# Seven products over whole contraction halves, with weight operations of eight tiles

## The chip, the core and the metric

The kernel runs on one core of a Trainium2 chip. The metric is the time on the device in microseconds, the median of the runs.

## What is computed

One step of a decoder layer on 512 prompt tokens and 8 sample tokens (520 columns in all, `TC`). The normalised input is projected by one wide matrix, and two branches read the result: dilated window attention (three groups of eight heads of 128) and chunkwise retention (eight heads, keys and values of 256). Their outputs are gated, projected, merged, projected again, normed and added to the residual; then comes a gated per-layer embedding. All is float32.

```python
u = rms_norm(h, g_pre)
z = jnp.einsum('bsd,de->bse', u, w_in)                 # 2048 x 22528
qa, ka, va, za, qr, kr, vr, zr, ga, gb = jnp.split(z, split_points, axis=-1)
...
merged = (jax.nn.sigmoid(ga) * jnp.einsum('bse,ed->bsd', ya, w_a_out)
          + jax.nn.sigmoid(gb) * jnp.einsum('bse,ed->bsd', yr, w_r_out))
y = jnp.einsum('bsd,de->bse', merged, w_o)
h = h + rms_norm(y, g_post)
h = h + jax.nn.sigmoid(jnp.einsum('bsd,de->bse', h, w_ple_gate)) * jnp.einsum('bsp,pd->bsd', p, w_ple_proj)
```

## The kernel before

**Splitting.** Every float32 operand of a matmul is split into a high part, rounded to the type that TensorE multiplies (`F32R`), and a low part, the rest. A product takes three passes: high by high, high by low, low by high. ScalarE makes the high part of the weights with a copy (`hi`, line 1004), VectorE the low part by subtraction (`lo`, line 1395). The moving operand (`U`, `V`) is split once for each stage.

**Pairs and operations.** The projections run over pairs of column blocks of 128 (`pairs`): five pairs a head for attention (numbers 0 to 39: q0 q1, k0 k1, q2 k2, v0 v1, v2 z), four a head for retention (q, k, v, gate z), sixteen for the gates, then the plain stages (`w_a`, `w_r`, `w_o`, the embedding's projection and gate). A pair is a list of operations (`OPS`); each is a weight tile of 4 x 128 columns that `hi` and `lo` split into one of `AHEAD` = 6 slots of `W`, and that TensorE then uses. SyncE loads the raw weights of a pair into `raw`, one buffer for one pair, in two halves of the contraction (`load`, lines 488 and 492); a half is loaded again when the low part of the last operation that reads it has been made.

**Seven products.** An `S` pair multiplies a 2 x 2 block form in seven products in place of eight (two column blocks by two halves of the 520 columns, and two parts of the contraction). Here this form covers the contraction's second half alone: tiles 8 to 11 against 12 to 15. Operations 0 to 6 are the seven products, 12 matmuls of 260 columns each; operations 7 to 10 are the first half in the plain form, 24 matmuls each: 180 in all, where a plain pair (`F`, `N`) has 192. Sums of weights are made by VectorE (lines 1390, 1392, 1399, 1402), sums of the moving operand once, at the start. ScalarE copies three partial results out of the accumulator (`part`, line 1061); VectorE adds them when it evicts the tiles (lines 1470, 1503).

**Order.** Each engine's order is written out by hand. For each operation n of a pair, VectorE and ScalarE run `steps`: what must be evicted, then the side work hung on that step (`hooks`), then `lo` or `hi` of the operation `AHEAD` places on. TensorE runs its own hooks ahead of the product of the same number: transposes, scores, values. Side work on VectorE includes the sample tokens' key products (`sample_keys`, lines 1640, 1643), softmax maxima and normalisation, state updates of the samples (`sample_states`, from line 1767), the retention's output (`ret_output`, from line 1821) and sample value columns (`sample_columns`, line 1734). GpSimd issues the loads and stores of the stages. SyncE issues the weight loads and, after each pair's, one or two copies of cache rows of 1 MB.

## Time and profile before

| | us |
|---|---|
| runs | 2926.57, 2930.59, 2932.53 |
| median | 2930.59 |
| span of the profiled execution | 2924.6 |
| attention pairs, about | 33.5 to 1000 |
| retention pairs, about | 1000 to 1866 |
| gate pairs | 1866 to 2223.6 |
| plain stages | 2223.6 to 2924.6 |

The profiled execution's own time is not given beside its span; the lowest run is 2.0 us above the span, the median 6.0. A row of the profile names the source line, the engine (PE is TensorE, PEld its weight load, DVE VectorE, ACT ScalarE, POOL GpSimd, SP SyncE; a q stands for the sequencer that issues or waits), the operation, what it writes and reads, and the shape. Where an idle time is shown, the arrow names what ended it.

### The profile page before, as it was taken

Reading aid. Unit: us, or ns where it says so; the run is one execution under the profiler, and the core shown is the slowest. Engines: PE = TensorE matmul, PEld = TensorE weight load, DVE = VectorE, ACT = ScalarE, POOL = GpSimd, SP = SyncE. Lnnn points to the kernel's source line nnn. Section 1 sums busy time; section 2 is a strip of 40 time slices with the busy share of each in tenths; the row PEclk is TensorE's granted clock in tenths of the full one; section 3 lists DMA queues with packets and bytes.
Section 4 is the critical chain, followed back from the end, with each engine's and each line's share of the span. In section 5 each row is a group of like instructions: output and inputs, shape, how many; then the busy total and the mean of one; then the engine's idle time right before and its main releaser. Section 6 shows DMA issues by size and latency. Waiting matters only on the chain.

```text
span 2924.6 us, 57340 instructions
## 1 busy us (share of the span) xinstructions
PE 2881.1 (99%) x23566; PEld 2843.2 (97%) x23566; DVE 1761.6 (60%) x3199; ACT 1143.6 (39%) x2078; POOL 350.1 (12%) x516
## 2 busy tenths in 40 slices
PE   7999999999999999999999999999999999999998
PEld 7999999999999999999999999999999999999998
DVE  6666667667666666576666667666654433433732
ACT  5444444444344434434434434433443322333432
POOL 2010000100001002112112112110001100000300
PEclk9999999999999999999999999999999999999999
DMA  8465655656556455456456456577568755553442
GB/s 273 129 211 172 216 169 186 212 163 198 185 186 200 150 173 189 152 202 224 140 200 223 143 197 223 171 271 261 203 230 311 245 195 203 213 184 137 159 163 95
DMA packets 375886, 567.16 MB, mean 194 GB/s; under 512 B 16112, under 2 KB 336432, under 8 KB 372416
## 3 DMA queue, kind: packets, MB, share of 16 engines
q1 hardware_dynamic: 334440, 428.38, 42.6%
q0 software_dynamic: 41184, 135.10, 14.9%
q8 instruction: 187, 3.06, 0.4%
q14 instruction: 75, 0.61, 0.1%
HBM read 511.42 MB, written 228.16 MB: 253 GB/s over the span
## 4 chain that ended last, share of the span: by engine, by line
PE 90%; DVE 4%; DMA 3%; DVEq 1%; ACT 1%; issue 1%; SPq 0%; POOL 0%; ACTq 0%; POOLq 0%
PE acc L546 58%; PE acc L558 21%; PE aux L756 1%; DMA raw_weights<-in_w_in 1%; PE aux L767 1%; DVE weights L1395 1%; PE aux L777 1%; PE aux L844 1%; PE aux L651 1%; DMA stage_buffers<-in_x_prompt 1%; PE aux L712 0%; PE aux L659 0%; DVE stage_buffers L2007 0%; PE aux L681 0%; PE aux L834 0%
## 5 line engine op out<-in xcount | busy, mean ns | idle before, releaser
L546 PE MATMUL acc<-moving,weights 128*128 128x260 f32 x12384 | 1566.1, 284 | 1.9 <-DVE sampled L1470 1.7
L546 PEld LDWEIGHTS acc<-moving,weights 128*128 128x128 f32 x12384 | 1509.4, 188 | 9.7 <-issue 6.1
L1395 DVE TENSOR_TENSOR weights<-raw_weights,weights 128x512 fp32r<-128x512 f32 (+1 forms) x1030 | 709.6, 694 | 599.3 <-ACT weights L1004 562.1
L1004 ACT ACTIVATE weights<-raw_weights 128x512 fp32r<-128x512 f32 (+1 forms) x1030 | 641.1, 626 | 1073.1 <-PE acc L546 439.5
L558 PE MATMUL acc<-moving,weights 128*128 128x260 f32 x5376 | 654.1, 284 | 6.1 <-DVE moving L1458 4.0
L558 PEld LDWEIGHTS acc<-moving,weights 128*128 128x128 f32 x5376 | 650.2, 189 | 6.4 <-issue 4.1
L546 PE MATMUL acc<-combined_moving,weights 128*128 128x260 f32 x3096 | 422.5, 286 | 0.8 <-DVE partial_sums L1503 0.8
L546 PEld LDWEIGHTS acc<-combined_moving,weights 128*128 128x128 f32 x3096 | 389.0, 189 | 1.4 <-DVE weights L1395 1.0
L1470 DVE SCALAR_TENSOR_TENSOR stage_buffers<-acc,partial_sums 128x260 f32<-128x260 f32 x344 | 146.6, 479 | 172.4 <-PE acc L546 172.4
L1004 ACT ACTIVATE weights<-combined_weights 128x512 fp32r<-128x512 f32 x172 | 108.1, 629 | 298.1 <-PE acc L546 268.9
L1061 ACT ACTIVATE partial_sums<-acc 128x260 f32<-128x260 f32 x258 | 99.7, 386 | 239.4 <-PE acc L546 234.3
L1395 DVE TENSOR_TENSOR weights<-combined_weights,weights 128x512 fp32r<-128x512 f32 x172 | 118.5, 689 | 118.5 <-ACT weights L1004 116.8
L2061 POOL DMA_DIRECT2D out<-stage_buffers x70 | 48.2, 689 | 870.9 <-ACTq L1074 657.1
L1390 DVE TENSOR_TENSOR combined_weights<-raw_weights 128x512 f32<-128x512 f32 x86 | 59.6, 693 | 51.9 <-DMA raw_weights<-in_w_in 45.3
L2138 POOL DMA_DIRECT2D out<-stage_buffers x64 | 45.7, 718 | 265.3 <-DVEq L1778 257.7
L1402 DVE TENSOR_TENSOR raw_weights<-raw_weights,combined_weights 128x512 f32<-128x512 f32 x86 | 59.5, 692 | 8.7 <-issue 0.9
L1392 DVE TENSOR_TENSOR raw_weights<-raw_weights 128x512 f32<-128x512 f32 x86 | 59.5, 692 | 8.4 <-issue 0.4
L1399 DVE TENSOR_TENSOR combined_weights<-combined_weights,raw_weights 128x512 f32<-128x512 f32 x86 | 59.5, 692 | 8.0
L2128 POOL DMA_DIRECT2D stage_buffers<-in_state_ret x64 | 45.6, 717 | 127.8 <-DVEq L1784 59.7
L1767 DVE SCALAR_TENSOR_TENSOR stage_buffers<-stage_buffers,sampled 128x256 f32<-128x256 f32 x128 | 53.4, 479 | 1.0
L2247 POOL TENSOR_TENSOR stage_buffers<-stage_buffers 128x520 f32<-128x520 f32 x16 | 24.3, 1520 | 224.8 <-DVE stage_buffers L2007 224.8
L2088 POOL DMA_DIRECT2D stage_buffers<-in_cache_win x24 | 21.7, 904 | 228.2 <-DVE sample_keep L1643 148.8
(264 smaller groups left out, 1873.2 us busy)
## 6 DMA issues: line engine op xcount, KB each, us to landing
out<-in_cache_win SPq DMA_DIRECT2D x128, 1023.5 KB, 8.8
raw_weights<-in_w_in SPq DMA_DIRECT2D x96, 1024.0 KB, 5.9
raw_weights<-in_w_in SPq DMA_DIRECT2D x160, 512.0 KB, 5.3
out<-in_cache_win SPq DMA_DIRECT2D x32, 1022.0 KB, 9.1
out<-stage_buffers POOLq DMA_DIRECT2D x120, 256.0 KB, 3.0
stage_buffers<-in_cache_win POOLq DMA_DIRECT2D x48, 512.0 KB, 5.6
stage_buffers<-in_state_ret POOLq DMA_DIRECT2D x64, 256.0 KB, 4.4
raw_weights<-in_w_r_out SPq DMA_DIRECT2D x16, 1024.0 KB, 5.6
```

The costliest lines, as they stand in the source:

```text
L546: mm = pe.matmul(acc[:, m, half, 0:HC], W[:, g % AHEAD, wp, kk, :], mov(up, kk), start=(start and kk == 0 and n == 0), stop=(stop and kk = ...
L558: mm = pe.matmul(acc[:, m, half, 0:HC], W[:, g % AHEAD, wp, kk, :], moving(first, half)(up, kk), start=(start and kk == 0 and n == 0), sto ...
L1004: act.activation(W[:, g % AHEAD, 0, 0:src.shape[1]], src, ACT.Copy).then_inc(s_whi, 1)
L1061: act.activation(part[:, i, :], acc[:, m, 1, 0:HC], ACT.Copy, scale=scale_of(p)).then_inc(s_read, 1)
L1390: dve.tensor_tensor(tmp_w[:], raw_chunk(2, 0), raw_chunk(3, 0), ALU.add).then_inc(s_sum, 1)
L1392: dve.tensor_tensor(raw_chunk(2, 0), raw_chunk(2, 1), raw_chunk(2, 0), ALU.subtract).then_inc(s_sum, 1)
L1395: dve.tensor_tensor(W[:, g % AHEAD, 1, 0:src.shape[1]], src, W[:, g % AHEAD, 0, 0:src.shape[1]].bitcast(F32), ALU.subtract).then_inc(s_wre ...
L1399: dve.tensor_tensor(tmp_w[:], tmp_w[:], raw_chunk(2, 1), ALU.subtract).then_inc(s_sum, 1)
L1402: dve.tensor_tensor(raw_chunk(3, 1), raw_chunk(3, 1), tmp_w[:], ALU.subtract).then_inc(s_sum, 1)
L1470: return dve.scalar_tensor_tensor(out=out, in0=bank, scalar=scale, in1=other_part, op0=ALU.mult, op1=ALU.add)
L1767: dve.scalar_tensor_tensor(out=r_st[:, slot, b, j, :], in0=r_v[:, slot, b, :], scalar=zs[:, at:at + 1], in1=r_st[:, slot, b, j, :], op0=AL ...
L2061: pool.dma_start(dst, src).then_inc(stored, 16)
```

## The change

The seven-product form of an `S` pair covers the whole contraction: tiles 0 to 7 against 8 to 15. A pair has seven operations of eight tiles, 24 matmuls each, 168 in all; the four plain operations go. The third pair of head 0 becomes plain (`N`), since the sums of the moving operand, now twice as large, are made in the first three pairs.

Every weight operation, in the plain stages too, is of 8 x 128 = 1024 columns; `AHEAD` is 3. `hi` waits for the high part of its slot to be used (`s_hused`) and `lo` for the whole slot. TensorE runs the sixteen matmuls with the high part first, and then waits for the low part. The sums of weights are made in place, in the raw buffer, one after each of the first four low parts. The raw buffer is loaded in four units (half, column block), each when its last reader is done.

VectorE evicts each accumulator when it is complete, in steps 4, 5 and 6. The hooks are moved to the seven (or four) steps that are left. The moving tiles are made in the order 0 to 15 (before: 8 to 15 first), and the first pair reads all eight tiles of a half in each operation. The stage buffers shrink from 15,824 to 12,804 columns: turned probabilities overwrite the probabilities, the attention output its gate, the retention's rows and outputs their sources, two key buffers serve for three. The scratch space for DMA descriptors is set to 4096 bytes. In the embedding's projection an operation serves four output tiles, in the first two pairs of its gate two.

```diff
-OPS = {"S": [("raw", 2, 1), ("raw", 2, 0), ("sum", 0), ("raw", 3, 1), ("sum", 0), ("raw", 3, 1), ("raw", 3, 0),
-             ("raw", 0, 0), ("raw", 1, 0), ("raw", 0, 1), ("raw", 1, 1)],
-       "N": [("raw", c, m) for m in range(2) for c in range(4)],
-       "Q": [("quad", c, t) for c in range(2) for t in range(4)],
-       "F": [("raw", c, m) for c in (2, 3, 0, 1) for m in range(2)],
-       "P": [("two", n // 8, n % 8) for n in range(KD)],
-       "A0": [("raw", c, m) for m in range(2) for c in (0, 1)],
-       "A1": [("raw", c, m) for m in range(2) for c in (2, 3)]}
-AHEAD = 6
+EIGHT = 8
+OPS = {"S": [(0, 1), (0, 1), (0, 0), (0, 1), (0, 1), (1, 0), (1, 1)],
+       "F": [(0, 0), (0, 1), (1, 0), (1, 1)],
+       "N": [(0, 0), (1, 0), (0, 1), (1, 1)],
+       "Q": [(0, 0), (0, 1), (1, 0), (1, 1)],
+       "P": [(0, 0), (0, 1), (1, 0), (1, 1)],
+       "A0": [(0, 0), (0, 1)],
+       "A1": [(1, 0), (1, 1)]}
+AHEAD = 3
...
-            add_pair("F" if h == 0 and j < 2 else "S", w_in, cols)
+            add_pair("FNN"[j] if h == 0 and j < 3 else "S", w_in, cols)
...
-    W = stack.enter_context(nc.sbuf_tensor("weights", [P, AHEAD, 2, 4, P], F32R))
+    W = stack.enter_context(nc.sbuf_tensor("weights", [P, AHEAD, 2, EIGHT, P], F32R))
...
-    POOL_F = 15824
...
+    POOL_F = 12804
...
-    V = stack.enter_context(nc.sbuf_tensor("combined_moving", [P, 2, 3, 4, HC], F32R))
-    tmp_w = stack.enter_context(nc.sbuf_tensor("combined_weights", [P, 4, P], F32))
+    V = stack.enter_context(nc.sbuf_tensor("combined_moving", [P, 2, 3, EIGHT, HC], F32R))
...
+    ya_out = silu_z[:, 0:T]
...
+    LAST_READ = {"S": {unit(0, 0): 2, unit(0, 1): 4, unit(1, 0): 5, unit(1, 1): 6},
...
+        def load(p, u):
+
+            half, m = divmod(u, 2)
+            if read_until[p.nth, u] >= 0:
+                sp.wait_ge(s_wready, read_until[p.nth, u] + 1)
...
+            sp.dma_start(chunk(half, m), rows[:, :, p.cols[m]:p.cols[m] + P]).then_inc(s_wload[u], 16)
...
         def product(g, m, half, mov, start, stop):
 
-            for kk in range(4):
-                for n, (wp, up) in enumerate(passes):
-                    mm = pe.matmul(acc[:, m, half, 0:HC], W[:, g % AHEAD, wp, kk, :], mov(up, kk),
-                                   start=(start and kk == 0 and n == 0), stop=(stop and kk == 3 and n == 2),
-                                   skip_group_check=True)
-            return mm
+            out = acc[:, m, half, 0:HC]
+            pe.wait_ge(s_whi, g + 1)
+            for kk in range(EIGHT):
+                for up in range(2):
+                    mm = pe.matmul(out, W[:, g % AHEAD, 0, kk, :], mov(up, kk), start=(start and kk == 0 and up == 0),
+                                   stop=False, skip_group_check=True)
+            mm.then_inc(s_hused, 1)
+            pe.wait_ge(s_wready, g + 1)
+            for kk in range(EIGHT):
+                mm = pe.matmul(out, W[:, g % AHEAD, 1, kk, :], mov(0, kk), start=False, stop=(stop and kk == EIGHT - 1),
+                               skip_group_check=True)
+            mm.then_inc(s_used, 1)
...
+            n = run(0)
+            if first:
+                pe.wait_ge(s_accfree[0], 1 + p.nth)
+            else:
+                pe.wait_ge(s_bankfree, p.sums)
+            product(n, 0, 1, moving(0, 0), True, False)
+            n = run(1)
+            acc_ready(0)
+            if first:
+                pe.wait_ge(s_comb, 4)
+            product(n, 0, 0, combined(1), True, False)
+            n = run(2)
+            acc_ready(1)
+            if first:
+                pe.wait_ge(s_comb, 8)
+            product(n, 1, 1, moving(0, 1), True, False)
+            n = run(3)
+            pe.wait_ge(s_read, 3 * p.sums + 1)
+            product(n, 0, 1, combined(0), False, True)
+            n = run(4)
+            pe.wait_ge(s_read, 3 * p.sums + 2)
+            product(n, 1, 1, moving(8, 1), False, True)
+            n = run(5)
+            pe.wait_ge(s_read7, p.sums + 1)
+            product(n, 0, 0, combined(2), False, True)
+            n = run(6)
+            product(n, 1, 0, moving(8, 0), True, True)
...
-            src = source(g)
-            act.activation(W[:, g % AHEAD, 0, 0:src.shape[1]], src, ACT.Copy).then_inc(s_whi, 1)
+                act.wait_ge(s_wready, g - AHEAD + 1)
+                act.wait_ge(s_hused, g - AHEAD + 1)
+            for u in units_read(p, n):
+                act.wait_ge(s_wload[u], loads_due[p.nth, u])
+            if p.mode == "S" and 1 <= n <= 4:
+                act.wait_ge(s_sum, 4 * p.sums + n)
+            act.activation(slot(g, W[:, g % AHEAD, 0]), source(g), ACT.Copy).then_inc(s_whi, 1)
...
+                hi(g + n + AHEAD)
+                if p.mode == "S" and n in (0, 2, 3):
                     act.wait_ge(s_used, g + n + 1)
                     if n == 0:
                         act.wait_ge(s_accfree[1], 1 + p.nth)
-                    i, m = {0: (1, 0), 2: (0, 1), 4: (2, 0)}[n]
+                    i, m = {0: (1, 0), 2: (0, 1), 3: (2, 0)}[n]
                     act.activation(part[:, i, :], acc[:, m, 1, 0:HC], ACT.Copy, scale=scale_of(p)).then_inc(s_read, 1)
...
-            strassen = p.mode == "S"
-            if strassen and n == 0:
-                dve.wait_ge(s_wload[1], 16 * loads_due[p.nth, 1])
-                dve.drain()
-                dve.tensor_tensor(tmp_w[:], raw_chunk(2, 0), raw_chunk(3, 0), ALU.add).then_inc(s_sum, 1)
-                dve.drain()
-                dve.tensor_tensor(raw_chunk(2, 0), raw_chunk(2, 1), raw_chunk(2, 0), ALU.subtract).then_inc(s_sum, 1)
-            src = source(g)
+            if g >= AHEAD:
+                dve.wait_ge(s_used, g - AHEAD + 1)
             dve.wait_ge(s_whi, g + 1)
-            dve.tensor_tensor(W[:, g % AHEAD, 1, 0:src.shape[1]], src, W[:, g % AHEAD, 0, 0:src.shape[1]].bitcast(F32),
+            dve.tensor_tensor(slot(g, W[:, g % AHEAD, 1]), source(g), slot(g, W[:, g % AHEAD, 0]).bitcast(F32),
                               ALU.subtract).then_inc(s_wready, 1)
-            if strassen and n == 2:
-                dve.drain()
-                dve.tensor_tensor(tmp_w[:], tmp_w[:], raw_chunk(2, 1), ALU.subtract).then_inc(s_sum, 1)
-            if strassen and n == 3:
-                dve.drain()
-                dve.tensor_tensor(raw_chunk(3, 1), raw_chunk(3, 1), tmp_w[:], ALU.subtract).then_inc(s_sum, 1)
+            if p.mode == "S":
+                weight_sums(p, n)
+
+        def weight_sums(p, n):
+
+            first, other = chunk(0, 1), chunk(0, 0)
+            if n == 0:
+                dve.wait_ge(s_wload[unit(0, 0)], loads_due[p.nth, unit(0, 0)])
+                dve.tensor_tensor(first, first, other, ALU.subtract).then_inc(s_sum, 1)
+            if n == 1:
+                dve.wait_ge(s_wload[unit(1, 0)], loads_due[p.nth, unit(1, 0)])
+                dve.tensor_tensor(other, other, chunk(1, 0), ALU.add).then_inc(s_sum, 1)
+            if n == 2:
+                dve.tensor_tensor(first, chunk(1, 0), first, ALU.subtract).then_inc(s_sum, 1)
+            if n == 3:
+                dve.wait_ge(s_wload[unit(1, 1)], loads_due[p.nth, unit(1, 1)])
+                dve.tensor_tensor(first, chunk(1, 1), first, ALU.subtract).then_inc(s_sum, 1)
...
+                    if n == 4:
+                        dve.wait_ge(s_read, 3 * s + 3)
+                        dve.wait_ge(s_read7, s + 1)
+                        evict(p, 0, 1, tiles[0], scale).then_inc(s_bankfree, 1)
+                    if n == 5:
+                        dve.wait_ge(s_used, g + 5)
+                        evict(p, 1, 1, tiles[1], scale)
+                    if n == 6:
+                        dve.wait_ge(s_used, g + 6)
+                        tile_ready(p, 0, tiles[0], scale)
...
+                if p.mode == "S" and n == 6:
+                    dve.wait_ge(s_used, g + 7)
+                    tile_ready(p, 1, tiles[1], scale)
+                lo(g + n + AHEAD)
...
+            return {(1, 0): [lambda: sample_states(0, h)], (1, 4): [lambda: sample_ret_y(0, h), lambda: sample_states(1, h)],
+                    (2, 0): [lambda: sample_ret_y(1, h)], (2, 1): [lambda: sample_states(2, h)], (2, 4): [lambda: sample_ret_y(2, h)],
+                    (3, 2): [lambda: sample_states(3, h)], (3, 6): [lambda: sample_ret_y(3, h)]}
...
-    nc = bacc.Bacc("TRN2", target_bir_lowering=False, num_devices=1)
+    nc = bacc.Bacc("TRN2", target_bir_lowering=False, num_devices=1, dynamic_dma_scratch_size=4096)
```

## Rows read from the trace of the kernel before

**Rows 1.** Page, part 1: span; each engine's busy time, share, instructions.

```profile
span 2924.6 us, 57340 instructions
PE 2881.1 (99%) x23566; PEld 2843.2 (97%) x23566; DVE 1761.6 (60%) x3199; ACT 1143.6 (39%) x2078; POOL 350.1 (12%) x516
```

**Rows 2.** Page, part 4: chain that ended last, shares by engine.

```profile
PE 90%; DVE 4%; DMA 3%; DVEq 1%; ACT 1%; issue 1%; SPq 0%; POOL 0%; ACTq 0%; POOLq 0%
```

**Rows 3.** Windows: length, busy PE, PEld, DVE, ACT, POOL; clock, DMA share, GB/s.

```profile
276.00:396.57 120.57, 120.57 (x1007) 120.26 (x1006) 79.25 (x144) 51.50 (x103) 9.41 (x14) 1.00 0.60 188
...
1648.80:1757.55 108.75, 108.41 (x860) 104.59 (x859) 75.31 (x152) 41.46 (x72) 21.64 (x32) 1.00 0.56 189
...
1866.00:2223.60 357.60, 357.06 (x2988) 356.65 (x2987) 224.53 (x402) 152.91 (x274) 33.34 (x49) 1.00 0.67 238
```

**Rows 4.** Windows of line 546 alone (PE, PEld): five gate pairs.

```profile
2115.91:2223.64 107.73, 107.73 (x902) 107.69 (x900) 1.00 0.62 225
```

**Rows 5.** Timeline, first projection: start us, length us, engine, line, operation, idle before.

```profile
32.74 0.69 DVE L1458 TENSOR_TENSOR moving<-stage_buffers,moving 128x520 fp32r<-128x520 f32 x1
...
33.58 26.60 PE L558 MATMUL acc<-moving,weights 128*128 128x260 f32 x206 [4.00 <-DVE moving L1458]
...
34.02 0.69 DVE L1458 TENSOR_TENSOR moving<-stage_buffers,moving 128x520 fp32r<-128x520 f32 x1
```

**Rows 6.** VectorE groups by shape: count, busy us, mean ns, idle before.

```profile
L1395 DVE TENSOR_TENSOR weights<-raw_weights,weights 128x512 fp32r<-128x512 f32 x1014 | 699.8, 695 | 590.9 <-ACT weights L1004 554.1 <-issue 0.7
...
L1640 DVE TENSOR_TENSOR stage_buffers<-stage_buffers 128x1024 f32<-128x1024 f32 x24 | 29.3, 1221 | 1.1
...
L1470 DVE SCALAR_TENSOR_TENSOR stage_buffers<-acc,partial_sums 128x260 f32<-128x260 f32 x298 | 125.5, 457 | 172.4 <-PE acc L546 172.4
```

**Rows 7.** ScalarE groups by shape, same columns.

```profile
L1004 ACT ACTIVATE weights<-raw_weights 128x512 fp32r<-128x512 f32 x1014 | 634.5, 629 | 1064.4 <-PE acc L546 439.5 <-PE acc L558 348.3 <-DVE raw_weights L1392 130.1
...
L1122 ACT ACTIVATE combined_moving<-stage_buffers 128x1040 fp32r<-128x1040 f32 x3 | 3.2, 1065 | 1.2 <-DVEq L1535 1.2
...
L1145 ACT ACTIVATE stage_buffers<-stage_buffers,sample_keep 128x1024 f32<-128x1024 f32 x32 | 36.5, 1141 | 17.0 <-DMA stage_buffers<-vrow_scr 17.0
```

**Rows 8.** The same timeline in one attention pair.

```profile
312.68 0.69 DVE L1392 TENSOR_TENSOR raw_weights<-raw_weights 128x512 f32<-128x512 f32 x1
...
313.29 0.68 DVE L1395 TENSOR_TENSOR weights<-raw_weights,weights 128x512 fp32r<-128x512 f32 x1
...
313.48 0.63 ACT L1004 ACTIVATE weights<-raw_weights 128x512 fp32r<-128x512 f32 x1 [0.97 <-DVE raw_weights L1392]
...
314.15 0.69 DVE L1395 TENSOR_TENSOR weights<-raw_weights,weights 128x512 fp32r<-128x512 f32 x1 [0.18 <-ACT weights L1004]
```

**Rows 9.** Loads: L492 at 86.0, at 305.1, all; L488, 1000 to 1866.

```profile
DMA to landing us min/median/max: 4.1/4.1/4.1
...
DMA to landing us min/median/max: 4.9/4.9/4.9
...
DMA to landing us min/median/max: 3.8/5.3/17.9
...
DMA to landing us min/median/max: 4.9/6.3/12.2
```

**Rows 10.** The same timeline: VectorE in a retention head.

```profile
1665.51 0.68 DVE L1821 COPY stage_buffers<-aux 128x512 f32<-128x512 f32 x1
...
1669.01 0.69 DVE L1395 TENSOR_TENSOR weights<-combined_weights,weights 128x512 fp32r<-128x512 f32 x1
...
1675.28 1.67 DVE L1767 SCALAR_TENSOR_TENSOR stage_buffers<-stage_buffers,sampled 128x256 f32<-128x256 f32 x4
...
1678.71 1.29 DVE L1395 TENSOR_TENSOR weights<-raw_weights,weights 128x512 fp32r<-128x512 f32 x2
...
1735.71 2.35 DVE L1734 TENSOR_TENSOR stage_buffers<-stage_buffers,sample_keep 128x1024 f32<-128x1024 f32 x2
...
1739.49 0.69 DVE L1395 TENSOR_TENSOR weights<-raw_weights,weights 128x512 fp32r<-128x512 f32 x1
```

755 lines of the change are left out of this document (377 added, 378 removed).

## The prediction

> **What bounds the kernel now.** I read the page's busy times first, then the chain of waits, then windows by stage, and last the single instructions around one pair of column blocks. TensorE is busy 99% of the span [rows 1] and carries 90% of the chain that ended last [rows 2]. Its clock is granted in full (1.00, the 2.4 GHz level) in an attention head, a retention head and the gate stage [rows 3]. Five gate pairs in a row without other TensorE work take 107.73 us for 900 matmuls [rows 4]: 0.1197 us a matmul, 21.55 us a pair of 180. So today a matmul removed is time removed. VectorE is busy 66% of an attention head and 69% of a retention head [rows 3]. The question is what becomes of that reserve when each weight operation grows to 1024 columns and half as many are held ahead.
>
> **The removed matmuls.** Before: 86 S pairs of 180 matmuls and 2 F pairs of 192, 15,864 in all. After: 85 S pairs of 7 x 24 = 168 and 3 plain pairs of 192, 14,856. That is 1,008 fewer, and 1,008 x 0.1197 = 120.7 us if TensorE stays the bound. A gate pair would then take 20.1 us. By the same rate five attention pairs (120.57 us before) come to 113.4, four retention pairs (108.75) to 103.0, sixteen gate pairs (357.6) to 334.6 [rows 3]. The matmuls of the later plain stages stay the same in number.
>
> **The first pair.** Tiles of the moving operand come every 1.28 us while the first projection runs (32.74 to 34.02) [rows 5]. Today each group of four tiles is used twice before the next is wanted, and the pair ends near 58.4 (192 of the 206 matmuls of the row that begins at 33.58). Afterwards the first operation wants eight tiles at once. The eighth is there at 33.4 + 7 x 1.28 = 42.4; its last two matmul pairs and the 16 low-part matmuls end at 44.8; three operations of 48 x 0.1197 = 5.75 follow, which find the sixteenth tile (52.6) in time: 62.0. Cost: 3.6 us.
>
> **The new loop.** The weight buffer holds one pair, and the four sums now stand in a line: each overwrites what the operation before has read. Between two pairs there is a closed loop. The low part of operation 4 ends, so the block of half 0, column 1 may be loaded for the next pair; then its high part (ScalarE), low part (VectorE), first sum (VectorE), high part, low part, second sum, and so on, to the low part of operation 4 again. That is one load, 5 high parts, 5 low parts, 4 sums. Today the loop holds a load too, but operations of 512 columns (0.63 and 0.69 us [rows 6, 7]), and the long products of half 0 cover it.
>
> The prices: a VectorE operation over 1024 columns 1.22 us (line 1640) [rows 6]; a ScalarE copy of 1040 columns into the rounded type 1.07 us, one of 1024 with a scale in place 1.14 [rows 7] (I take 1.06, being of the first kind, and keep 1.14 as the bound); a low part followed by a sum overlaps by 0.08 (312.68 + 0.69 against 313.29); from VectorE's end to ScalarE's start 0.11, back 0.04 [rows 8]. A load of 512 KB alone lands in 4.1 us, beside a cache copy in 4.9; the median of all is 5.3, but half of those stand behind another [rows 9]. I take 4.4, nearest to the undisturbed one, and keep 4.1 and 5.3. Sum: 4.4 + 5 x 1.06 + 9 x 1.22 - 4 x 0.08 + 6 x 0.11 + 5 x 0.04 = 21.2 us a pair, between 20.9 and 22.5. It lies above the 20.1 of a gate pair and just under the 21.55 of today: in the gates the loop takes nearly all of the gain. The Trainium skill (DMA: Bandwidth & Descriptors, Anatomy of one DMA) fits, for the software path, 2.0 us plus bytes over 436 GB/s, an estimated 3.2 us for such a load, which would make the loop 20.0 and leave TensorE the bound; the row's 4.1 speaks against it.
>
> **What else VectorE does in the loop.** While ScalarE makes a high part, VectorE is free for 0.11 + 1.06 + 0.04 = 1.21 us, four times a pair; two of these gaps are taken up by evictions (0.46 us each and more, line 1470) [rows 6]. While the load runs, it is free for about 5.6 us less two low parts and two evictions, 2.4 us. Side work that does not fit its gap lengthens the loop.
> - Attention, a head: a sample-key product and reduction, 2 x 1.22, in one gap: 1.2 over. Two bursts of about 5 us (maxima with a key product; exchange with normalisation, an estimate from the 1024-column price) in the load's gap: 2 x 2.6. Small things 1: in all 7.4. Loop 5 x 21.2 + 7.4 = 113.4, TensorE 113.4. Two bounds as close as that do not meet in every pair, since VectorE can run ahead of TensorE by two products at most; I take 115.5, 5.1 less than before. Seven heads: -36. Head 0: two S pairs -2; its third pair becomes plain, +1.4.
> - Retention, a head [rows 10]: a state update is 3.4 us (1675.28 to 1678.71): 2.2 over in an empty gap, 3.5 with scaled keys beside it, 1.2 in the load's gap. The output step is 3.5 (1665.51 to 1669.01) in a gap that evictions have filled: 3.4 over. Update and sample columns, 3.4 + 3.8 (1735.71 to 1739.49), in the load's gap: 4.8. The last columns 2.5. In all 17.6. Loads of 1 MB in this stage land in 6.3 where undisturbed ones take 4.9 [rows 9]; half of that, 0.7, for each half-size load. Loop 4 x 21.9 + 17.6 = 105.2, TensorE 103.0; with the same lack of fit 106, 2.7 less than before. Eight heads: -22.
> - Gates: 16 x 21.2 + 21 (one output step 3.4, four updates 5, columns 8, the closing tiles 5) = 360, 3 more than before.
>
> **Edits with one answer.** SyncE issues four loads of half the size for a pair; what waits behind them are cache copies, for which nothing waits before the end. The copies of partial sums on ScalarE now follow the next high part: product 4 starts one high part and one copy (1.5 us) after its own high part, which fits, as TensorE has 1 us a pair to spare where the loop binds and is not late where it doesn't. The denser stage buffers (turned probabilities and outputs over their sources, two key buffers for three) wait for stores that end a pair or more earlier; nothing where GpSimd keeps up, and it is busy 12% of the span [rows 1]; up to 2 us a head if one store is late. Less room for GpSimd's DMA descriptors shows in no row; I take nothing.
>
> **Sum.** -36 - 2 + 1.4 - 22 + 3 + 3.6 = -52. The profiled span is 2924.6; the three runs lie 2.0 to 7.9 above it, their median 6.0. So 2872.6 + 6.0 = 2879 us, 1.8% faster.
>
> **Rivals.**
> - *TensorE stays the bound.* Loads that land sooner once each has the queue to itself, and side work that fits better than I count, give -120.7 + 3.6 = -117: 2813. For it: loop and TensorE differ by only one us a pair. Against: the 4.1 us.
> - *The loop is longer and the kernel slower.* At the upper prices (load 5.3, high part 1.14) the loop is 22.5: attention 5 x 22.5 + 7.4 = 120 a head (nothing won), retention 4 x 23.2 + 17.6 = 110.4 (+1.6 x 8 = 13), gates 16 x 22.5 + 21 = 381 (+23), start +3.6: about +40, 2970. It decides from about 21.8 us a pair, 0.6 above my price: 52 us over 83 S pairs. For it: one weight buffer, so that each microsecond of a load is paid in the loop, and loads in this program wait for one another. The Trainium skill (Trainium Kernel Development and Optimization, Best Practices) says to double-buffer so that DMA overlaps with compute; this change loads into a buffer that the last sums have only just left, and by that rule this rival is what happens.
> - *Late stores*: the buffers shared in the stages cost 2 us in each of 16 heads on top of the forecast, 2911: still faster.
>
> **How the numbers follow.** Chances: forecast 0.47 (2850 to 2915), TensorE the bound 0.22, longer loop 0.21, late stores 0.10. The range takes in the first rival and part of the second: 2811 to 2945. A measurement tells about 0.2% (6 us) from no change. Faster: the forecast, the first rival and the third, less a little at the edge, 0.76; within 0.2%, the loop near 21.8, 0.06; slower 0.18.
>
> **What would show it.** If I am right, gate pairs without side work take about 21 us, TensorE waits there about a microsecond a pair for ScalarE's high parts, and ScalarE's longest waits are for the weight load and for VectorE's sums. Attention pairs lose about 1 us each, retention pairs 0.7. The first pair ends near 62. If TensorE stays the bound, gate pairs take 20.1 and nothing waits. If the loop is longer, gate pairs take over 21.6. I am wrong about the loop if the load is not waited for, or if ScalarE's 1024-column copy or VectorE's operations are not near 1.06 and 1.22 us.

## The result, and the profile after

The change made the kernel slower. The changed kernel takes 3071.6 us (median of 4 runs, 3071.3 to 3072.9), the kernel before, run beside it, 2929.6: a ratio of 1.0486 [1.0471, 1.0501], 142 us more. The prediction had said 2879, with a range that ended at 2945.

The page of the changed kernel (busy times, then the chain that ended last) answers [rows 1, 2]:

```profile
span 3069.6 us, 54404 instructions
PE 2845.6 (93%) x22558; PEld 2779.5 (91%) x22558; DVE 1992.9 (65%) x2727; ACT 1158.6 (38%) x1600; POOL 350.5 (11%) x517
...
PE 49%; DVE 23%; ACT 9%; DMA 6%; DVEq 6%; issue 6%; ACTq 1%; POOL 1%; SPq 0%; POOLq 0%
```

The 1,008 matmuls are gone (23,566 to 22,558 instructions). But TensorE now stands idle for 3069.6 - 2845.6 = 224 us, where it was 43.5, and carries 49% of the chain that ended last, where it was 90%. Its busy time fell by 35.5 us and not by the 120.7 of the removed matmuls. Of the other 85 us at most some 64 are work done at the lower clock (1.2 GHz): TensorE is busy for 138 us in the stretches granted that level, for 10 before, and half of the difference is the most that it can cost. The rest must be short waits inside rows that count as busy: the gate pairs below are busy for 82.55 us at a clock of 1.00, where the same matmuls take 80.64 in a later run. Windows (columns as in [rows 3]): an attention head, that head's second pair (called j1 from here on; the pairs of a head are j0, j1 and so on), a retention head, the gates, and four gate pairs without side work:

```profile
543.76:670.43 126.67, 115.69 (x947) 114.79 (x946) 93.48 (x124) 53.55 (x82) 9.41 (x14) 0.97 0.58 182
568.81:598.49 29.68, 21.08 (x175) 20.88 (x173) 21.42 (x25) 9.18 (x11) 2.89 (x4) 0.92 0.72 205
1644.46:1761.05 116.59, 107.32 (x811) 101.22 (x810) 87.46 (x136) 43.52 (x57) 21.63 (x32) 0.96 0.56 176
1990.40:2360.10 369.70, 348.67 (x2831) 342.54 (x2830) 264.14 (x334) 159.92 (x212) 34.10 (x50) 1.00 0.68 230
...
2251.07:2335.83 84.76, 82.55 (x674) 81.09 (x673) 58.87 (x64) 36.53 (x49) 2.86 (x4) 1.00 0.66 224
```

Undisturbed gate pairs take 84.76 / 4 = 21.19 us, the 21.2 of the forecast. The attention head, though, went from 120.6 to 126.7, the retention head from 108.8 to 116.6, the gates from 357.6 to 369.7 [rows 3] (their window is laid 5 us early), and in the heads the granted clock is 0.96 or 0.97 on average. By stages, each from its first product to the next one's, attention takes 1018.6 us, retention 943.2, the gates 369.8 and the plain stages 704.3: about 52, 77, 12 and 3 more than before. The forecast had -33, -22, +3 and 0, so retention missed by some 99 us and attention by 85. What TensorE waited for, the largest four (us in total, times, longest):

```profile
PE aux L689 <- DVEq L1560: 72.0, 15, 8.9
PE aux L805 <- DVE sample_keep L1859: 35.3, 7, 5.5
PE aux L786 <- DVEq L1560: 21.0, 7, 8.1
PE aux L882 <- DVEq L1855: 14.7, 18, 2.4
```

None of them is a product of the projections. They are transposes of an evicted tile (L689 in attention, L786 in retention), the second values product of retention (L805) and its products with the sampled states (L882), each waiting for VectorE. The longest, at the end of that attention pair j1, in the timeline of all engines:

```profile
575.59 1.22 DVE L1471 TENSOR_TENSOR raw_weights<-raw_weights 128x1024 f32<-128x1024 f32 x1
576.72 1.22 DVE L1713 TENSOR_TENSOR stage_buffers<-stage_buffers 128x1024 f32<-128x1024 f32 x1
578.02 1.22 DVE L1716 TENSOR_REDUCE sample_keep<-stage_buffers 128x8 f32<-128x1024 f32 x1
579.15 2.35 DVE L1453 TENSOR_TENSOR weights<-raw_weights,weights 128x1024 fp32r<-128x1024 f32 x2
...
588.86 1.23 DVE L1713 TENSOR_TENSOR stage_buffers<-stage_buffers 128x1024 f32<-128x1024 f32 x1 [5.47 <-DMA stage_buffers<-row_scr]
...
589.98 1.06 ACT L1056 ACTIVATE weights<-raw_weights 128x1024 fp32r<-128x1024 f32 x1 [9.03 <-DMA raw_weights<-in_w_in]
...
597.72 1.11 PE L689 MATMUL aux<-ident,stage_buffers 128*128 128x128 f32 x4 [8.60 <-DVEq L1560]
598.49 3.20 PE L575 MATMUL acc<-moving,weights 128*128 128x260 f32 x16
```

Two things wait for a DMA at once. VectorE waits 5.47 us for the second set of sample keys (L1713), and ScalarE waits 9.03 us for the next pair's weights (L1056). Both loads were let go by VectorE within 1.2 us of each other: the reduction at 578.02 frees the key buffer, the remainder at 579.15 (that is, a low part) frees the weights' block. The issues of 577 to 583, KB each, median us to landing:

```profile
raw_weights<-in_w_in SPq DMA_DIRECT2D x2, 512.0 KB, 9.7
stage_buffers<-in_cache_win POOLq DMA_DIRECT2D x1, 512.0 KB, 6.6
```

9.7 is the median of two weight loads; the first, issued at 580.39, is the one that ScalarE waits for and took 9.5 us. I had it at 4.4, 5.3 at most. After such a gap the first 16 matmuls take 3.20 us, where 2.09 to 2.17 is usual in this trace.

### The profile page after: what moved, and what is told of

Read it like the earlier page. It is cut to its first block, busy times and chain, and to the rows that moved or that the text cites. A ratio compares the mean times of both kernels' runs of the same rounds, so it can differ in the third digit from the quotient of the medians.

```text
span 3069.6 us, 54404 instructions
## 1 busy us (share of the span) xinstructions
PE 2845.6 (93%) x22558; PEld 2779.5 (91%) x22558; DVE 1992.9 (65%) x2727; ACT 1158.6 (38%) x1600; POOL 350.5 (11%) x517
## 3 DMA queue, kind: packets, MB, share of 16 engines
q1 hardware_dynamic: 488360, 428.39, 43.5%
## 4 chain that ended last, share of the span: by engine, by line
PE 49%; DVE 23%; ACT 9%; DMA 6%; DVEq 6%; issue 6%; ACTq 1%; POOL 1%; SPq 0%; POOLq 0%
PE acc L575 14%; PE acc L592 13%; DVE weights L1453 11%; ACT weights L1056 7%; PE acc L598 7%; PE acc L580 6%; DMA raw_weights<-in_w_in 3%; DVEq L1560 3%; DVE raw_weights L1463 2%; DMA stage_buffers<-row_scr 2%; DVE stage_buffers L1533 1%; PE aux L805 1%; DVE raw_weights L1471 1%; DVE raw_weights L1468 1%; PE aux L815 1%
## 5 line engine op out<-in xcount | busy, mean ns | idle before, releaser
L1453 DVE TENSOR_TENSOR weights<-raw_weights,weights 128x1024 fp32r<-128x1024 f32 x723 | 884.6, 1226 | 851.7 <-ACT weights L1056 489.4
L1056 ACT ACTIVATE weights<-raw_weights 128x1024 fp32r<-128x1024 f32 x723 | 761.7, 1058 | 1647.0 <-PE acc L592 318.8
L575 PE MATMUL acc<-moving,weights 128*128 128x260 f32 x5440 | 750.0, 292 | 11.5 <-ACT partial_sums L1114 11.4
L575 PEld LDWEIGHTS acc<-moving,weights 128*128 128x128 f32 x5440 | 703.5, 195 | 18.2 <-ACT partial_sums L1114 15.0
L575 PE MATMUL acc<-combined_moving,weights 128*128 128x260 f32 x4080 | 544.4, 286 | 8.2 <-DVE stage_buffers L1533 5.1
L575 PEld LDWEIGHTS acc<-combined_moving,weights 128*128 128x128 f32 x4080 | 508.5, 189 | 11.2 <-DVE stage_buffers L1533 7.0
L592 PE MATMUL acc<-moving,weights 128*128 128x260 f32 x3712 | 473.3, 286 | 14.0 <-DVE stage_buffers L1533 7.7
L592 PEld LDWEIGHTS acc<-moving,weights 128*128 128x128 f32 x3712 | 457.4, 190 | 16.7 <-DVE stage_buffers L1533 7.9
L580 PE MATMUL acc<-moving,weights 128*128 128x260 f32 x2720 | 387.8, 286 | 0.0
L580 PEld LDWEIGHTS acc<-moving,weights 128*128 128x128 f32 x2720 | 356.6, 192 | 0.0
L580 PE MATMUL acc<-combined_moving,weights 128*128 128x260 f32 x2040 | 286.6, 283 | 0.0
L580 PEld LDWEIGHTS acc<-combined_moving,weights 128*128 128x128 f32 x2040 | 262.9, 189 | 0.0
L598 PE MATMUL acc<-moving,weights 128*128 128x260 f32 x1856 | 242.5, 283 | 0.0
L598 PEld LDWEIGHTS acc<-moving,weights 128*128 128x128 f32 x1856 | 232.1, 189 | 0.0
L1533 DVE SCALAR_TENSOR_TENSOR stage_buffers<-acc,partial_sums 128x260 f32<-128x260 f32 (+1 forms) x340 | 160.9, 473 | 79.9 <-PE acc L580 70.1
L2146 POOL DMA_DIRECT2D out<-stage_buffers x70 | 48.3, 690 | 944.9 <-ACTq L1123 711.9
L1466 DVE TENSOR_TENSOR raw_weights<-raw_weights 128x1024 f32<-128x1024 f32 x85 | 103.5, 1218 | 5.2 <-DMA raw_weights<-in_w_in 5.2
L1471 DVE TENSOR_TENSOR raw_weights<-raw_weights 128x1024 f32<-128x1024 f32 x85 | 103.5, 1218 | 0.0
L1468 DVE TENSOR_TENSOR raw_weights<-raw_weights 128x1024 f32<-128x1024 f32 x85 | 103.5, 1218 | 0.0
L1463 DVE TENSOR_TENSOR raw_weights<-raw_weights 128x1024 f32<-128x1024 f32 x85 | 103.5, 1218 | 0.0
L689 PE MATMUL aux<-ident,stage_buffers 128*128 128x128 f32 x192 | 34.0, 306 | 72.7 <-DVEq L1560 72.0
```

The source lines that it names most:

```text
L575: mm = pe.matmul(out, W[:, g % AHEAD, 0, kk, :], mov(up, kk), start=(start and kk == 0 and up == 0), stop=False, skip_group_check=True)
L580: mm = pe.matmul(out, W[:, g % AHEAD, 1, kk, :], mov(0, kk), start=False, stop=(stop and kk == EIGHT - 1), skip_group_check=True)
L592: mm = pe.matmul(acc[:, m, half, 0:HC], W[:, g % AHEAD, 0, kk, :], moving(first, half)(up, kk), start=(start and kk == 0 and up == 0), sto ...
L598: mm = pe.matmul(acc[:, m, half, 0:HC], W[:, g % AHEAD, 1, kk, :], moving(first, half)(0, kk), start=False, stop=(stop and kk == EIGHT - 1 ...
L1056: act.activation(slot(g, W[:, g % AHEAD, 0]), source(g), ACT.Copy).then_inc(s_whi, 1)
L1453: dve.tensor_tensor(slot(g, W[:, g % AHEAD, 1]), source(g), slot(g, W[:, g % AHEAD, 0]).bitcast(F32), ALU.subtract).then_inc(s_wready, 1)
```

## The experiments

Two theories stood at the start. **A**: what was added stands in VectorE's queue (the key product behind its wait, then weight operations, then the evictions), and TensorE's side work waits for its end. **B**: the closed chain of the weights (load, rounding on ScalarE, remainder and sum on VectorE, again rounding) sets the pairs. After four runs B was worked out as **D**: a pair takes the chain's 21.3 us plus whatever lengthens one of its links.

**Key products moved apart.** In VectorE's tables, attention:

```diff
-                {1: [lambda: sample_keys(0, h - 1)], 4: [lambda: sample_keys(1, h - 1)]} if h else
+                {1: [lambda: sample_keys(0, h - 1)]} if h else
...
-                 3: [lambda: sample_keys(2, h - 1)], 5: [lambda: masked_far(1, h)]} if h else
+                {0: [lambda: sample_keys(1, h - 1)], 1: [lambda: masked_near(0, h)],
...
-                {**({} if h else {0: [first_lo], 2: [lambda: masked_far(1, h)]}),
+                {**({0: [lambda: sample_keys(2, h - 1)]} if h else {0: [first_lo], 2: [lambda: masked_far(1, h)]}),
```

> The changed kernel with one thing moved: VectorE's second key product of each attention head goes from step 4 of the key pair (j1) to step 0 of the next pair (j2), the third from step 3 of j2 to step 0 of j3, so that some six steps lie between two products that share one buffer, where there were three. Theory A (what was added stands in VectorE's queue: it waits 4 to 6 us for the key load, the next pair's weight operations and the evictions stand behind that wait, and TensorE's transposes at step 0 of j2 wait 8 us for an eviction): TensorE's wait there falls from 8 us to under 1 us in each of 7 heads (-50 us), the half clock that follows it goes too (-20 us), pair j1 falls from 29.1 to 21.5-22.5 us, the time from 3072 to about 3000 (2985-3020). Theory B (the closed chain of load, rounding, remainder and sum sets the pairs, wherever the key products stand): pairs as before the move, 3072 within 0.3%. Theory C (the wait only moves along, to j2 or j3): j1 gets shorter by 7, j2 and j3 together longer by 4 or more, about 3045.

Measured: 3078.9 us (two runs, 3072.1 and 3085.8). TensorE's wait stayed:

```profile
PE aux L689 <- DVEq L1560: 74.4, 15, 9.0
```

VectorE no longer waits for keys in j1, yet nothing is won. The wait that I had read off first, the 5.47 us, was not the one that counted: ScalarE's 9 us for the weights end 1.1 us later, and with the keys out of the way the wait for the weights is still there (9.47 us in the same head). Theory A fell for attention.

**State products read early.** In TensorE's table and in VectorE's:

```diff
-                    (2, 3): [lambda: sample_states(0)], (3, 5): [lambda: sample_states(1)]}
+                    (2, 3): [lambda: sample_states(0)], (3, 4): [lambda: sample_states(1)]}
...
-                    (3, 2): [lambda: sample_states(3, h)], (3, 6): [lambda: sample_ret_y(3, h)]}
+                    (3, 2): [lambda: sample_states(3, h)], (3, 4): [lambda: sample_ret_y(3, h)]}
```

> The changed kernel with one thing moved: in retention's fourth pair (j3) TensorE's products with the sampled states go from step 5 to step 4 and VectorE's copy of them out of the bank from step 6 to step 4. Theory A (TensorE's second values product at step 6 waits 5 us for that copy, which stands behind two remainders and two sums of the next pair's weights on VectorE): the wait goes from 5.0 to under 1 us in 7 heads (-35 us), the half clock behind it goes (-15 us), pair j3 falls from 36.2 to 29-31 us, the time from 3072 to about 3022 (3005-3040). Theory B (the closed weight chain sets j3): unchanged within 0.3%. Theory C (TensorE waits for the next thing in VectorE's queue in its place, the sampled rows or the value columns): j3 falls by under 2 us, over 3055.

Measured: 3026.5 us, -45. The same j3 in windows of the changed kernel and of this one:

```profile
1723.88:1761.05 37.17, 32.05 (x220) 28.80 (x219) 24.71 (x33) 11.16 (x16) 3.25 (x5) 0.91 0.37 116
```

```profile
1701.00:1731.07 30.07, 30.07 (x221) 27.88 (x220) 24.74 (x33) 11.18 (x16) 3.17 (x5) 1.00 0.45 140
```

The wait at L805 is gone, TensorE is busy without a break, and the clock is back at the upper level. This third of the loss was a hook's place: VectorE freed bank 3 at step 6, behind two remainders and two sums of the next pair, and TensorE wanted it at step 6. Here A holds.

**Both moves.**

> Both moves of the two runs before together. Theory A: the gains add, -70 and -50: about 2952 (2925-2990), so that most of the 142 us that the change lost, or all of it, is gone with no weight operation removed. Theory B: 3072. If only one of the two waits cost time: 3000 or 3022.

Measured: 3029.4 us (ratio to before 1.0341 [1.0323, 1.0358]): the second move's gain and nothing from the first.

**TensorE kept busy in the wait.** Before the wait of the transposes at step 0 of j2:

```diff
+            for _ in range(75):
+                pe.transpose(aux[:, 3, 0:P], ident[:], ident[:])
             pe.wait_ge(s_zT, tiles)
```

> The changed kernel with 75 transposes of the unit matrix (about 6.9 us by 0.092 us each) into a free bank in front of TensorE's wait at step 0 of the attention pair j2, heads 1 to 7; nothing else is changed, and their result is overwritten. They fill the 8 us in which TensorE stands idle. If the half clock after the gap is a consequence of the idle engine (theory A): the granted clock stays at 1.0 behind the wait, the some 7 us at half clock per head cost 3.4 us less, 7 x 3.4 = 24: about 3048 (3040-3058). If the half clock has another cause, or costs nothing because VectorE sets the pace there: 3072 within 0.3%. If the transposes reach beyond the wait: up to +5 us.

Measured: 3068.5 us (two runs), -3, hardly more than the noise. The same place, one head:

```profile
582.79 7.70 PE L689 MATMUL aux<-ident 128*128 128x128 f32 x69
590.36 0.66 PE L692 MATMUL aux<-ident,stage_buffers 128*128 128x128 f32 x4
590.77 2.17 PE L575 MATMUL acc<-moving,weights 128*128 128x260 f32 x16
```

The 16 matmuls behind the wait take 2.17 us in place of 3.20, so here the half clock does follow the idle engine. But it is worth 3 us and not 24. In the profiled execution j2 became 1.6 us shorter in each head and attention 10 us in all; retention and the gates, where nothing was changed, took 5 us more. That the rest is lost because VectorE sets the pace there fits, but is not shown. Only the gaps at this one place were filled: the stretches at the lower level fell from 209 to 164 us.

**Key load held back.** GpSimd issues the second key load only when five of the pair's seven products are done; VectorE's key products at (j1, 1), (j2, 3), (j3, 2).

```diff
             pool.wait_ge(s_skfree, count.due(s_skfree))
+            if g == 1:
+                pool.wait_ge(s_used, pairs[ATT + 5 * (h + 1) + 1 if h + 1 < H else RET + 1].first + 5)
```

> The changed kernel, with the load of the second set of sample keys held back until five of the seven products of its pair are done (a wait on GpSimd, in front of its DMA issue), and VectorE's key products at step 1 of j1, step 3 of j2 and step 2 of j3, so that each finds its keys loaded. Theory D, formed after the first four runs: the weights of a pair go round a closed chain (load of unit 0,1: 4.3 us; rounding and first remainder 2.4; four times remainder, rounding and sum: 3.64 each; 21.3 us in all) and whatever makes one link longer makes the pair longer. In attention the keys' load (two DMAs of 512 KB) starts within 1 us of that weight load and both take 7 to 10 us. With the two apart the weight load of j2 goes from 8.7 to 4.3-4.8 us, TensorE's wait at step 0 of j2 from 8 to 3-4 us, j1 from 29.1 to 24.5-25.5; 8 heads: -32, half clock -10: about 3030 (3015-3045). Theory A (what stands in VectorE's queue, wherever the DMA stands): as with the key products moved alone, 3072-3079.

Measured: 3045.3 us, -26 (ratio to before 1.0393 [1.0372, 1.0414]). Pair j1 of the same head, and the weight loads between 569 and 574.5:

```profile
558.43:582.22 23.79, 20.73 (x174) 20.53 (x173) 18.88 (x23) 8.87 (x11) 1.46 (x2) 1.00 0.64 210
```

```profile
raw_weights<-in_w_in SPq DMA_DIRECT2D x3, 512.0 KB, 6.0
```

The pair falls from 29.68 to 23.79 us. The median of the three loads is 6.0; the first, which the chain waits for, lands in 4.07. Some of the gain is given back: j3 and j4 get 1.9 and 1.2 us longer, the pairs that have the moved key products and their loads in them now. So in attention it was two loads that collide, inside a chain that has nothing to hide the longer one.

**One rounding done twice.** In ScalarE's `hi`:

```diff
+            if p.mode == "S" and n == 1:
+                act.activation(slot(g, W[:, g % AHEAD, 0]), source(g), ACT.Copy)
+                act.drain()
             act.activation(slot(g, W[:, g % AHEAD, 0]), source(g), ACT.Copy).then_inc(s_whi, 1)
```

> The changed kernel with one rounding on ScalarE of each pair's seven done twice (1.06 us, and the wait between the two some 0.2 us): that of the second product, which is one of the chain's links. ScalarE has 62% of its time idle. Theory D: each pair that the chain sets gets 1.1 to 1.3 us longer: the gate pairs after the first (14), attention's j2 and j4 chains (15), retention's j2 (7), and retention's j3 in part; the chains of attention j0, j1, j3 and retention j0, j1 have 1.2 to 4.4 us of room between load and rounding and take it up: +40 to +50, about 3117 (3105-3130). If the chain set every pair: +1.2 x 85 = 3175. If TensorE's hooks and VectorE's queue set the pairs and not the chain (theory A): 3072 to 3080.

Measured: 3176.2 us, +105. Four plain gate pairs, and TensorE's largest wait (72.0 us in the changed kernel):

```profile
2355.19:2443.66 88.47, 82.77 (x674) 81.11 (x673) 58.90 (x64) 39.86 (x52) 2.85 (x4) 1.00 0.61 207
```

```profile
PE aux L689 <- DVEq L1563: 103.1, 22, 11.6
```

They go from 84.76 to 88.47, 0.9 us each; over all, 105 / 85 = 1.2 us a pair. ScalarE is idle for more than half of the time, and yet work on one of its links is paid. That the mean equals the price of the added work is in part luck, since the pairs differ: retention's j0 (22.81 us in both kernels) and attention's j2 pay nothing, attention's j0 pays 1.1 us, and j1 and j3 of both stages pay 2.3 to 2.7, more than was added. There the waits of TensorE's transposes grow as well, and the stretches at the lower clock go from 209 to 338 us. The room of 1.2 to 4.4 us that I had counted on was there in retention's j0, not in attention's j0, j1, j3 or retention's j1. A likely reason is that every link also holds one of the three weight buffers, on which TensorE waits; their number was not varied.

**Retention's side work spread over more steps**, on top of the state products read early. The head's output is cut in three functions and the state update in two; VectorE's table becomes (TensorE's and ScalarE's follow):

```diff
+            return {(1, 0): [lambda: scaled_values(h)], (1, 1): [lambda: gated_values(h)],
+                    (1, 2): [lambda: state_products(0, h)], (1, 3): [lambda: state_rows(0, h)], (1, 5): [lambda: sample_ret_y(0, h)],
+                    (1, 6): [lambda: state_products(1, h)], (2, 0): [lambda: state_rows(1, h)], (2, 3): [lambda: sample_ret_y(1, h)],
...
```

> The kernel with the state products read early (3026) and, in retention, VectorE's side work spread: the head's output in three parts (step 6 of j0, steps 0 and 1 of j1; 0.8, 1.5 and 1.4 us) in place of one of 3.7 us; each of the four state updates of 3.3 us in two halves, two of the four in the steps 2 and 3, in which VectorE waits for the next weight load; TensorE's and ScalarE's parts of it moved along. No work is added or removed. Theory D: a link of the chain has 1.28 us in which VectorE waits for ScalarE anyway, so a piece up to that costs nothing, and a longer one its excess. The chain that ends in j1 goes from 30.3 to 24-26 us, that in j2 from 28.3 to 24-25: 8 to 10 us a head, 7 heads: -55 to -70: about 2965 (2950-2990). If TensorE's own hooks set these pairs: 3026 within 0.3%. If the moved parts make new waits on ScalarE or TensorE: above 3026.

Measured: 3063.3 us, 37 more than the 3026 it started from, where 60 less was expected. Waits of TensorE, 14.5 us at L882 and none at L872 before the move:

```profile
PE aux L882 <- DVEq L1859: 37.1, 21, 5.6
PE aux L872 <- DVE stage_buffers L1918: 13.9, 5, 3.0
```

Retention's j2 and j3 got 3.6 and 2.1 us longer, j1 only 0.5 shorter: TensorE's state products (L882) and sampled values (L872) now come directly behind the VectorE step that feeds them. Cutting side work in pieces moves its end, and someone waits for the end.

**States early, keys held back and side work spread.**

> The three moves together (states read early, key load held back, retention's side work spread). Theory D: the savings add, 3072 - 46 - 42 - 60 = about 2924 (2905-2955), level with the kernel before the change, 2930, with each of its operations still there and only their places changed. Theory A: about 3020.

Measured: 3035.5 us; the two gains and the loss add up.

**Two sums one remainder earlier.**

```diff
                 dve.tensor_tensor(first, first, other, ALU.subtract).then_inc(s_sum, 1)
-            if n == 1:
                 dve.wait_ge(s_wload[unit(1, 0)], loads_due[p.nth, unit(1, 0)])
                 dve.tensor_tensor(other, other, chunk(1, 0), ALU.add).then_inc(s_sum, 1)
-            if n == 2:
+            if n == 1:
                 dve.tensor_tensor(first, chunk(1, 0), first, ALU.subtract).then_inc(s_sum, 1)
```

> The changed kernel with two of VectorE's four weight sums of each pair put one remainder earlier in its order: the second directly behind the first (it needs neither the first sum nor the remainder between), the third directly behind the remainder of the product before it. Same operations, same number, same results. Theory D (the closed chain of load, rounding, remainder and sum sets the pace, 21.3 us and what is put into it): in three of the four links VectorE no longer waits 1.28 us for ScalarE's rounding, since a sum or a remainder runs beside it, so that the chain falls by 3 x 1.28 = 3.8 to about 17.5 us, below the 20.16 us of TensorE's own products; side work then has 2.7 us of room a pair. Gate pairs 23.1 -> 20.2-21.0 (-40 us), attention heads 127.4 -> 119-121 (-56), retention heads 118 -> 107-111 (-65): about 2910 (2870-2950), below the kernel before the change, 2930. Theory A (what costs is TensorE's hooks waiting for VectorE's queue, whose length this leaves): 3040-3072. If a load of the second half comes too late for the earlier sum: a gain of under half, 3000-3040.

Measured: 3049.3 us (ratio 1.0409 [1.0393, 1.0425]): -22, where 160 was expected; by the time alone this is theory A's range. Four plain gate pairs, a new wait of VectorE, and one of TensorE (21.0 us before the move):

```profile
2236.69:2317.33 80.64, 80.64 (x675) 80.64 (x674) 59.24 (x65) 37.21 (x49) 2.86 (x4) 1.00 0.70 237
```

```profile
DVE raw_weights L1465 <- DMA raw_weights<-in_w_in: 31.9, 11, 6.3
PE aux L786 <- DVEq L1559: 51.9, 7, 9.1
```

Where the chain alone sets the pace theory D is right: 20.16 us a pair, TensorE busy throughout. Attention gained 23 us and the gates 18, but in j1 of attention the colliding loads stay (27.0 us a pair on average). Retention lost 18: in six heads the earlier sum finds its load not there (22.8 of the 31.9 us), and the evictions behind it, for which the transposes at L786 wait, come late.

**Sums earlier and states early; then keys held back as well.**

> The run with the sums earlier, and the state products of retention's j3 read early as well. Theory D: the wait of TensorE at step 6 of j3 hung on two links of the chain; with these shorter it is 2 to 4 us before this move, and gone with it: 15 to 45 us below the run with the sums alone, about 2880 (2840-2925). If the shorter chain has already taken that wait away: the same as that run within 0.3%.

> The run with the sums earlier, the state products read early, and the key load held back as well. Theory D: with the chain at 17.5 us a weight load that takes 8.7 us in place of 4.3 makes it 21.9 and, with 2 to 3 us of side work, still longer than TensorE's 21 to 22 us in j1 by some 2 us; holding the keys back is worth 7 x 2 = 15 us against the run without it, less what the later keys cost in j3 and j4 (10 to 20 us in the run that moved them alone): level within 15 us, 2865-2895.

Measured: 3005.1 us, then 2951.9. The states are worth 44 again. Holding the keys back is worth 53 on the shorter chain, where it was 26 on the longer one, and I had expected it level within 15. The gain in attention's j1 is the same both times, 5 us a head; what differs is the cost of the moved key products in j3 and j4, 1.9 and 1.2 us a head on the longer chain, 0.4 and 0.2 on the shorter one, which has room for them.

**Retention mended as its trace asks**, on top of all three:

```diff
+        late_sums = {RET + 4 * h + 2 for h in range(1, H)} | {GATE + 2}
...
-            return {(1, 0): [lambda: sample_states(0, h)], (1, 4): [lambda: sample_ret_y(0, h), lambda: sample_states(1, h)],
-                    (2, 0): [lambda: sample_ret_y(1, h)], (2, 1): [lambda: sample_states(2, h)], (2, 4): [lambda: sample_ret_y(2, h)],
+            return {(1, 0): [lambda: sample_states(0, h)], (1, 3): [lambda: sample_states(1, h)], (1, 4): [lambda: sample_ret_y(0, h)],
+                    (2, 0): [lambda: sample_ret_y(1, h)], (2, 2): [lambda: sample_states(2, h)], (2, 5): [lambda: sample_ret_y(2, h)],
...
+                states_in(2, h - 1)
                 if h >= 2:
                     values_in(h - 2, 0)
                     values_in(h - 2, 1)
-                states_in(2, h - 1)
```

> The run with sums earlier, states read early and keys held back (2952), with retention mended as its trace asks: the second state update at step 3 of j1 in place of step 4, the third at step 2 of j2 in place of step 1 (both then behind the last link of the chain, in the time in which VectorE waits for the next weight load), TensorE's and VectorE's reading of the third one step later; GpSimd issues the sampled values' loads (two of 512 KB) behind the third state load, which moves them from step 1 to step 4 of j1, away from the weight loads; and the pair j2's second and third sums (and the third gate pair's) stay at their old places, since there the load of the second half was what VectorE waited for (5.3 us). Theory D: the chain that ends in j2, 33.0 us, loses 3.5 (third update), 2 to 3 (second) and 3 to 5 (late load): j1 from 32.5 to 24.5-27, 7 x 7 = -49, half clock -10: about 2895 (2870-2920), below the kernel before the change, 2930. If TensorE's hooks set j1 and j2 (transposes, scores, states): 2940-2952.

Measured: 2915.0 us (5 runs, 2913.3 to 2916.5); ratio to before 0.9949 [0.9936, 0.9963]. Its page and its largest waits of TensorE:

```profile
span 2911.5 us, 54412 instructions
...
PE 2795.0 (96%) x22558; PEld 2744.2 (94%) x22558; DVE 1983.6 (68%) x2727; ACT 1164.5 (40%) x1600; POOL 350.6 (12%) x517
```

```profile
PE aux L689 <- DVEq L1562: 26.4, 22, 2.0
PE aux L786 <- DVEq L1562: 16.1, 7, 2.6
```

It beats both kernels, with every matmul and weight operation of the change in it; only places in the order differ. Against the kernel before that is 0.5%, 16 us of the 120.7 that the removed matmuls are worth: attention takes 952 us and the gates 351, less than before, but retention takes 871, still some 5 us more. TensorE's idle time is 116.5 us, half of the 224, and still above the 43.5 of before.

**The sums put back there.**

> The fastest kernel so far (2915: sums earlier, states read early, keys held back, state updates and value loads moved) with the sums put back to their old places in every pair; the other moves stay. Moved alone, the sums were worth 22 us where theory D said 160. Either (theory D, mended) the chain's 1.28 us a link were paid for in full only where nothing else held the pair, and other waits hid the gain: then taking them back now, with those waits gone, costs much more than 22: gates +0.9 x 16, attention +5 a head (j0 0.7, j1 1.9, j2 0.8 and more), retention +1 a head: about +65, 2980 (2955-3000). Or the links matter little (the moves of loads and hooks did it all): +15 to +25, 2935.

Measured: 2987.2 us (ratio 1.0195 [1.0177, 1.0212]): +72. Nearly the same edit (the fastest kernel leaves the sums of eight pairs late) was worth 22 alone. Of the 50 us between, about 21 are in attention (44 here, 23 alone), all in j2 to j4, where the moved key products now stand and find room; about 29 are in retention, which lost 18 alone and now, with the sums of j2 left late, gains 11. In the gates it is 18 both times. So about 72 us of the way from 3072 to 2915 hang on the places of two sums in a pair, given the other moves.

**The kernel before, its chain made longer**, in its own `hi`:

```diff
+            if op_of[g][0].mode == "S" and op_of[g][1] in (2, 4):
+                act.activation(W[:, g % AHEAD, 0, 0:src.shape[1]], src, ACT.Copy)
+                act.drain()
             act.activation(W[:, g % AHEAD, 0, 0:src.shape[1]], src, ACT.Copy).then_inc(s_whi, 1)
```

> The kernel before the change with the same lengthening as the second rounding in the changed kernel (there 1.2 us on one link, +104 us in all, 1.2 us in each of 85 pairs): of each seven-product pair's eleven roundings of 512 columns two are done twice, those of two operations that read a weight sum, 2 x 0.63 us and the waits between, some 1.6 us a pair on ScalarE. Theory D: six operations held ahead and products of unmixed weights between the sums leave TensorE the bound, and ScalarE's 61% idle time takes it up: 2930 to 2945. If the sums' chain sets the kernel before as well: +1.6 x 86 = 138, 3070.

Measured: 2929.0 us, ratio 0.9997 [0.9988, 1.0006]. The added copies:

```profile
L1005 ACT ACTIVATE weights<-combined_weights 128x512 fp32r<-128x512 f32 x172 | 108.1, 629 | 300.5 <-PE acc L546 269.0 <-DVE combined_weights L1402 29.3 <-PE acc L558 1.9
```

Two times 0.63 us of added ScalarE work a pair cost nothing there; one time 1.06 us a pair cost 105 in the changed kernel. The sensitivity came with the change. Which part of the change brought it (the sums made in place, one behind the other, or three operations of double size held ahead in place of six) was not tried apart.

## Why the prediction was wrong

- **Matmuls and their price**: right. Four pairs of 168 matmuls take 80.64 us where TensorE is the bound, 0.12 us each.
- **The first pair**: right within 1.2 us; the second projection begins at 63.2, where the first was to end at 62.0.
- **The new loop**: right in size. VectorE's 1024 columns 1.23 and 1.22 us, ScalarE's 1.06, undisturbed loads 3.8 to 4.3, in all 21.2 a pair in plain gate pairs. The Trainium skill's fit for the software path (DMA: Bandwidth & Descriptors, Anatomy of one DMA) gives an estimated 3.2 us for such a load. The trace disagrees for these loads, which go by SyncE's queue: the shortest of the 352 loads of `w_in` took 3.6.
- **What else VectorE does in the loop**: the step that failed. It took 115.5 us for an attention head, 106 for a retention head and 360 for the gates; measured were 126.7, 116.6 and 369.7. Beyond the bare loop of 21.2 us a pair it had priced 9.5 us a head in attention and 21.2 in retention, and 20.7 and 31.8 were needed. Three things are behind it. The load was priced at 4.4 us in attention, and the one in j1 took 9.5, because a key load is let go in the same moment [the run with the key load held back: j1 from 29.7 to 23.8 us, -26 in all, -53 with a shorter chain]. No term was there for TensorE's own side work waiting for the end of VectorE's: the place of one such hook, in retention's j3, is worth 45 us alone. And what the loop can absorb was overrated: VectorE's 1.21 us beside each high part were counted as room for side work, and VectorE's running ahead by two products as a cushion, so that 2.1 us a head were added for the lack of fit. The doubled rounding shows little of a cushion (2.3 to 2.7 us for 1.06 in j1 and j3), and filling that time with two of the loop's own sums is worth 72 us in the fastest kernel. Retention's j1, 30 to 33 us in most heads, stays unexplained.
- Two slips in the working change nothing: the time free beside the load is by its own terms 2.2 us, not 2.4, and the S pairs are 85, not 83.
- **Edits with one answer**: the list has no term for the moved hooks. A step to which they were moved is 24 matmuls, 2.87 us, and VectorE does up to two operations of 1.2 us of the next pair in one; the wait at L805 stood behind two such steps.
- **The rival on the slower side** (loop of 22.5, 2970) named the right place, one weight buffer in which each microsecond of a load is paid and loads that wait for one another; j1 in attention shows both. But it wanted a longer loop everywhere, and the plain loop stayed at 21.2, below the 21.8 from which it was to decide, while the time came out 102 us above its 2970. The Trainium skill advises to double-buffer (Trainium Kernel Development and Optimization, Best Practices); the 9.03 us for which ScalarE waited on a weight load agree with it. A second weight block was not tried.
- **TensorE stays the bound** (2813): within reach only of the gates, once the sums stand earlier. **Late stores**: no run isolates them.
- The half clock behind TensorE's gaps, some 64 us of busy time at most, stood in no term. In attention's j2 it is a consequence of the gap and costs little by itself: filling the gaps there gave 3 us. Elsewhere this was not tried.

What stays open: in the fastest kernel retention's j1 still takes 28 to 30 us against 22 for the same pair of the first head, which has neither state updates nor an earlier head's output to make; which of its side work to move next was not tried.

## What to carry to other kernels

When an edit turns a bound engine's slack into a closed chain through other engines, price not only the bare chain, which came out right here, but for each link what stands in front of it, who waits behind it, and which transfer starts beside its load. A quick test of whether an engine with much idle time stands in the chain that sets the pace is to do one of its operations twice: 0 us before, 105 us after. And a move that wins little alone may be worth much more beside others (22 and 72 us here: the shorter chain had room for the moved key products, and the pairs in which the move cost time were left out), so mend the waits in the order in which they end last, and measure moves together as well as alone.

## What the hardware showed

A weight load of 512 KB on SyncE's queue, issued 0.7 us after a key load of 512 KB on GpSimd's (whose second part of 512 KB followed 0.2 us later), landed after 9.5 us, the key load after 6.6; with the key load held back the same weight load took 4.07, and in the plain gate pairs a load that was alone in the queue 3.8 to 4.3. After an idle gap of 8.6 us TensorE ran at the lower level (1.2 GHz; granted clock 0.50 from 596 to 600 us, 1.00 from 605.5 on), 3.20 us for 16 matmuls that take 2.17; with transposes filling the gap it did not (granted clock 1.00).
